# Ranked routing, a written-out first expert iteration, and mixer outputs formed transposed in half lanes

## The reference

```python
e = exp(s - max(s)); o = (e / sum(e)) @ v              # each head, queries in blocks of 128
o_b = g0 * o_cmp + g1 * o_sel + g2 * o_win
merged = g_a*(o_a @ w_br_a) + g_b*(o_b @ w_br_b) + g_c*(o_c @ w_br_c)
```

## Time and profile before

| | us |
|---|---|
| median of 3 runs | 1678.88 |
| the profiled execution | 1675.22 |
| its span | 1673.5 |
| TensorE busy in it | 1590.7 (95%) |
| VectorE busy | 939.6 (56%) |
| ScalarE busy | 654.3 (39%) |
| mean granted TensorE clock | 0.988 |

### The profile page before, as it was taken

How to read it: one execution, slowest core, us unless ns; L and a number is a source line. 1 busy time by engine, 2 the same in 40 slices (tenths; PEclk the granted TensorE clock), 3 DMA queues, 4 the chain that set the end, 5 groups by cost and what they waited for, 6 DMA issues and landing times.

```text
span 1673.5 us, 22371 instructions
## 1 busy us (share of the span) xinstructions
PE 1590.7 (95%) x9359; PEld 1237.3 (74%) x9359; DVE 939.6 (56%) x1374; ACT 654.3 (39%) x960; POOL 27.1 (2%) x89
## 2 busy tenths in 40 slices
PE   5999999989999899999999999999999999999998
PEld 1998655454545377687888899978768878889986
DVE  3876676642222465556675566545466567556653
ACT  2543411111111243556545544335265744543441
POOL 1000010100000000000000000000000000000000
PEclk9999999999999999999999999999999999999999
DMA  9555519979999943333345355545424235435551
GB/s 309 189 186 201 202 52 332 386 289 414 411 423 381 353 142 129 102 137 109 133 152 180 123 192 172 191 154 192 154 76 152 101 130 191 157 130 185 202 181 71
DMA packets 153155, 333.33 MB, mean 199 GB/s; under 512 B 17764, under 2 KB 69222, under 8 KB 140774
## 3 DMA queue, kind: packets, MB, share of 16 engines
q1 hardware_dynamic: 147504, 326.94, 53.9%
q10 hardware_dynamic: 5558, 5.06, 0.9%
HBM read 330.94 MB, written 1.05 MB: 198 GB/s over the span
## 4 chain that ended last, share of the span: by engine, by line
PE 81%; DVE 9%; DMA 4%; ACT 4%; issue 1%; POOL 0%; ACTq 0%; POOLq 0%; DVEq 0%; SPq 0%
PE ps_g L737 19%; PE ps_g L718 15%; PE ps_g L1142 6%; PE ps_g L1282 6%; PE ps_s L1538 4%; PE ps_p L1538 3%; PE ps_o L785 3%; PE ps_g L878 3%; DVE ring_r L2314 2%; PE ps_p L718 2%; PE ps_o L1171 2%; DMA ring<-in_w_mod_dram 1%; PE ps_x L1171 1%; PE ps_p L775 1%; DMA arena<-in_w_up_dram 1%
## 5 line engine op out<-in xcount | busy, mean ns | idle before, releaser
L2314 DVE TENSOR_TENSOR ring_r<-ring,late_w 128x4096 fp32r<-128x4096 f32 (+1 forms) x50 | 216.9, 4339 | 153.3 <-ACT late_w L1876 153.3
L1876 ACT ACTIVATE late_w<-ring 128x4096 fp32r<-128x4096 f32 (+1 forms) x50 | 178.2, 3563 | 126.7 <-PE ps_p L1538 42.8
L737 PE MATMUL ps_g<-hf_high,ring_r 128*128 128x256 f32 x640 | 179.0, 280 | 0.0
L737 PE MATMUL ps_g<-hf_high,late_w 128*128 128x256 f32 x576 | 162.1, 281 | 0.0
L737 PE MATMUL ps_g<-h_t_r,late_w 128*128 128x256 f32 x576 | 161.3, 280 | 0.0
L737 PEld LDWEIGHTS ps_g<-hf_high,ring_r 128*128 128x128 f32 x640 | 122.0, 191 | 0.0
L737 PEld LDWEIGHTS ps_g<-h_t_r,late_w 128*128 128x128 f32 x576 | 108.6, 189 | 0.0
L737 PEld LDWEIGHTS ps_g<-hf_high,late_w 128*128 128x128 f32 x576 | 108.1, 188 | 0.0
L1900 ACT ACTIVATE arena<-arena,neg_max 128x256 f32<-128x256 f32 (+1 forms) x160 | 71.5, 450 | 40.9 <-DVE neg_max L2369 40.9
L1142 PE MATMUL ps_g<-arena 128*64 128x512 f32 x288 | 83.9, 592 | 0.0
L718 PE MATMUL ps_g<-early_w,first_low 128*128 128x512 f32 (+1 forms) x176 | 68.7, 390 | 3.8 <-ACT arena L1862 1.8
(11 more groups left out here) (697 smaller groups left out, 3707.1 us busy)
## 6 DMA issues: line engine op xcount, KB each, us to landing
ring<-in_w_in_dram SPq DMA_DIRECT2D x31, 2048.0 KB, 7.8
ring<-in_w_gate_up_dram SPq DMA_DIRECT2D x44, 1024.0 KB, 7.3
arena<-in_w_down_dram SPq DMA_DIRECT2D x16, 2048.0 KB, 13.1
ring<-in_w_mod_dram SPq DMA_DIRECT2D x10, 2048.0 KB, 11.0
ring<-in_w_down_dram SPq DMA_DIRECT2D x10, 2048.0 KB, 7.9
arena<-in_w_gate_dram SPq DMA_DIRECT2D x16, 1024.0 KB, 13.4
arena<-in_w_up_dram SPq DMA_DIRECT2D x8, 2048.0 KB, 16.1
ring<-in_w_gate_dram SPq DMA_DIRECT2D x8, 2048.0 KB, 14.2
```

Source lines behind the costliest of these rows:

```text
L737: ins = pe.matmul(b.ap[:, (f % 2) * SEQ:(f % 2 + 1) * SEQ], a[:, k, f * P:(f + 1) * P], x[:, k, :], start=k == 0 and i == 0, stop=k == nk ...
L1876: act.activation(high_of(name, rnd)[:, 0:n], ring[:, slot, 0:n], ACT.Copy).then_inc(high_ready.sem, 1)
L2314: dve.tensor_tensor(ring_r[:, slot, 0:n], ring[:, slot, 0:n], high_of(name, rnd)[:, 0:n].bitcast(F32), ALU.subtract).then_inc(low_ready.se ...
```

## The change

It has three parts.

**Routing.** Instead of three searches one after the other, every value is compared with every other of its four ("greater", and "equal" times a fixed mask `before` of earlier indices), and the sums are ranks. A group of rank 0 and experts of rank below 2 give `picked`. Gates are formed from rank 0 and rank 1 later. The slot row is made by a matmul of its own in bank O ahead of the h2 transposes and copied by DVE after `shifted`; loads go to bank G0. Modulation chunk 10 moves ahead of `mod_strips(7)` on PE (bank X) and is copied by ACT, its +1 now added as 1/128 in each partition; chunk 11 moves behind the first gather, and DVE takes it after the gates. ACT's exponential of the logit difference and 11 small DMA issues (`layer_vectors(0)`) move behind `take_tokens`.

**Expert pairs.** Pairs 0 and 1 are written out ahead of PE's loop; the register is loaded behind them. In `expert_pair` the waits for banks O and X stand before the gate products' k = 0 and k = 4, and that for M1 before the up products.

**Mixer outputs.** The output is formed transposed: the values are the stationary operand (64 columns, so half the lanes), the transposed probabilities are moving (128 columns). A second set of four matmuls spreads the reciprocals over the lanes. DVE copies those to SBUF, multiplies, and has the branch output transposed already (`heads_t`), so the 24 transposes go away; ACT and DVE make high and low parts from SBUF. For cmp the probabilities are scaled on DVE before PE transposes them.

```diff
+            claim(O, "slot_row")
+            pe.matmul(O.ap[:, 0:SLOT_TOKENS], ones, tri[:, 0:SLOT_TOKENS], start=True, stop=True).then_inc(O.full, 1)
             for tb in range(TB):
                 turn_block("h2", tb, ...)
...
             residual(1)
-            for i in MOD_LATE:
-                modulation(i)
             pe.wait_ge(picked_ready, 1)
             claim(X, "places")
...
             gather(0, "taken")
-            pe.wait_ge(rounds_ready, 1)
-            n_pairs = pe.value_load(rounds_i[0:1, 1:2], ...)
+            modulation(MOD_LATE[1])
...
-            with pe.Fori(0, last_even, 2) as q:
+            even_and_odd(0)
+            pe.wait_ge(rounds_ready, 1)
+            last_even = pe.value_load(rounds_i[0:1, 3:4], ...)
+            with pe.Fori(2, last_even, 2) as q:
                 even_and_odd(q)
...
                     if step[0] != "cmp":
                         turn_probs("layer", step, l)
                         return
-                    pe.wait_ge(probs.sem, probs.at("layer", step_tag(step), l))
+                    pe.wait_ge(blocks_scaled, len(CMP_STEPS) * l + CMP_STEPS.index(step) + 1)
                     claim(PT, step_tag(step), l)
...
+                def turned_output(step, v):
+                    tag, kbs = step_tag(step), keys_of(step) // P
+                    claim(O, tag, l)
+                    pe.wait_ge(PT.free, PT.nth("layer", tag, l))
+                    for c in range(2):
+                        for b in range(kbs):
+                            for half in range(2):
+                                pe.matmul(O.ap[half * HD:(half + 1) * HD, c * P:(c + 1) * P], v(2 * c + half, b), probs_t[:, 2 * c + half, b, :],
+                                          start=b == 0, stop=b == kbs - 1)
+                    pe.wait_ge(inverse_ready, len(WEIGHED) * l + WEIGHED.index(step) + 1)
+                    inverse = rden[:, MIXER_STEPS.index(step) % 2, 0:4]
+                    for i in range(4):
+                        half, c = i % 2, 2 + i // 2
+                        ins = pe.matmul(O.ap[half * HD:(half + 1) * HD, c * P:(c + 1) * P], inverse[:, i:i + 1].broadcast_to([P, HD]), ident[:, :],
+                                        start=True, stop=True)
+                    ins.then_inc(O.full, 1)
...
-                        pe.matmul(O.ap[:, :], probs_t[:, 0, 0, :], cmp_v[...], start=True, stop=True)
+                        for c in range(KF):
+                            ins = pe.matmul(O.ap[:, c * P:(c + 1) * P], v[:, c * P:(c + 1) * P], probs_t[:, 0, 0, :], start=True, stop=True)
...
             for tb in range(TB):
                 shifted(tb)
+            dve.wait_ge(O.full, O.nth("first", "slot_row"))
+            dve.tensor_copy(slot_row[:, 0, :], O.ap[:, 0:SLOT_TOKENS]).then_inc(O.free, 1)
...
-            first_best(rt[:, :, 0:N_GROUPS], 2, 8)
+            for op, over_groups, over_experts in ((ALU.is_gt, group_beats, beats), (ALU.is_equal, group_ties, ties)):
+                v = rt[:, :, 0:N_GROUPS]
+                st.done(dve.tensor_tensor(square(over_groups), each_row(v), each_column(v), op))
+                for tb in range(TB):
+                    v = of_experts(tb)
+                    st.done(dve.tensor_tensor(over_experts[:, tb]..., each_row(v), each_column(v), op))
+            st.settle()
+            ...                                   # ties times earlier (2), beats plus ties (2), sums (2), settled after each
+            do(dve.tensor_scalar(group_rank[:, :, :], group_rank[:, :, :], 0.5, None, ALU.is_lt))
+            do(dve.scalar_tensor_tensor(grouped(picked[:, :, :]), grouped(rank[:, :, :]), 1.5, chosen, ALU.is_lt, ALU.mult))
+            dve.sem_inc(picked_ready, 1)
...
+                    dve.tensor_tensor(block_scores(n), block_scores(n), over(rden[:, n % 2, :], CMP), ALU.mult).then_inc(blocks_scaled, 1)
...
+                def mixer_inverse(n):
+                    step = MIXER_STEPS[n]
+                    if step[0] == "cmp":
+                        total_blocks(n, step)
+                        return
+                    ...                           # waits for probs; sink added for swa; reciprocal; gate for sel, win
+                    ins.then_inc(inverse_ready, 1)
...
+                    dve.wait_ge(O.full, O.nth("layer", step_tag(step), l))
+                    sums, weight = (O.ap[:, i * SEQ:(i + 1) * SEQ].rearrange(...) for i in range(2))
+                    st.done(dve.tensor_copy(o_tmp[:, :, :], weight))
+                    st.settle()
+                    if step[0] != "win":
+                        dve.tensor_tensor(out_t, sums, o_tmp[:, :, :], ALU.mult).then_inc(O.free, 1)
+                        return
+                    ...                           # win: product to o_tmp, then added
...
                 for n, step in enumerate(MIXER_STEPS):
-                    if step[0] == "cmp":
-                        total_blocks(n, step)
+                    mixer_inverse(n)
                     if n + 2 < len(MIXER_STEPS):
                         mixer_mask(n + 2)
                     mixer_finish(n)
...
                 for name in "abc":
-                    turned_low(f"o{name}", KF, o_low[name], o_high[name], l)
+                    for r in range(2):
+                        dve.wait_ge(x_high.sem, x_high.at("layer", f"o{name}{r}", l))
+                        dve.tensor_tensor(o_low[name][:, 2 * r:2 * r + 2, :], heads_t[name][:, 2 * r:2 * r + 2, :],
+                                          o_high[name][:, 2 * r:2 * r + 2, :].bitcast(F32), ALU.subtract).then_inc(heads_low_ready, 1)
```

More of the change, by code:

```diff
@@ L627, in two_blocks @@
         g_col_ready, last_used = sem("g_col_ready"), sem("last_used")
+        inverse_ready, blocks_scaled, heads_low_ready = sem("inverse_ready"), sem("blocks_scaled"), sem("heads_low_ready")
+        WEIGHED = [step for step in MIXER_STEPS if step[0] != "cmp"]
         bg_tanhed, cmp_tanhed = sem("bg_tanhed"), sem("cmp_tanhed")
@@ L1120, in _ @@
                 b.begin("moe", n)
-            for b in (MO, MX):
-                pe.wait_ge(b.free, b.nth("start", "taken"))
-            last_even = pe.value_load(rounds_i[0:1, 3:4], min_val=PAIRS - 2, max_val=PAIRS * ROUNDS - 2)
             def expert_pair(q, gate_landed, gate_w, up_landed, up_w, last=False):
@@ L1131, in weights_of @@
                     return up_w[e]
-                for b in (MO, MX):
-                    pe.wait_ge(b.free, q * 2 + 1)
+                first = isinstance(q, int) and q == 0
                 claim(M0, "gate", q)
-                claim(M1, "up", q)
                 halves = [slice(e * SLOT_TOKENS, (e + 1) * SLOT_TOKENS) for e in range(2)]
@@ L1140, in expert_pair @@
                     for k in range(KD):
+                        if kind and k == 0:
+                            claim(M1, "up", q)
+                        if kind == 0 and k % 4 == 0:
+                            y = (MO, MX)[k // 4]
+                            pe.wait_ge(y.free, y.nth("start", "taken") if first else q * 2 + 1)
                         for lanes, w in zip(halves, both_w):
@@ L1373, in _ @@
                     mixer_output(n)
-                for name, src in (("a", o_a), ("b", o_b), ("c", o_c)):
-                    if name == "b":
-                        pe.wait_ge(rows.sem, rows.at("layer", "ob", l))
-                    else:
-                        pe.wait_ge(O.free, O.nth("layer", step_tag((SWA_STEPS if name == "a" else MLA_STEPS)[-1]), l))
-                    turn_rows(f"o{name}", [lambda tb, k=k, s=src: s[:, tb, k * P:(k + 1) * P] for k in range(KF)], l)
                 def mem_half(r):
@@ L2021, in _ @@
             copy_block("mg", 1, mg_turned)
-            for i in (6, 7):
-                keep_strips(i)
+            keep_strips(6)
+            b = mod_bank(MOD_LATE[0])
+            act.wait_ge(b.full, b.nth("first", MOD_CHUNKS[MOD_LATE[0]]))
+            act.activation(mod_cols(MOD_LATE[0]), b.ap[:, 0:HALF], ACT.Copy).then_inc(b.free, 1)
+            keep_strips(7)
             for i in (6, 7):
@@ L2211, in _ @@
                 for name in "abc":
-                    turned_high(f"o{name}", KF, o_high[name], l)
+                    if name == "b":
+                        act.wait_ge(rows.sem, rows.at("layer", "ob", l))
+                    else:
+                        act.wait_ge(O.free, O.nth("layer", step_tag((SWA_STEPS if name == "a" else MLA_STEPS)[-1]), l))
+                    for r in range(2):
+                        act.activation(o_high[name][:, 2 * r:2 * r + 2, :], heads_t[name][:, 2 * r:2 * r + 2, :], ACT.Copy).then_inc(x_high.sem, 1)
                 make_high("brb", l)
@@ L2803, in _ @@
                 shifted(tb)
-            dve.sem_inc(alpha_ready, 1)
+            dve.wait_ge(O.full, O.nth("first", "slot_row"))
+            dve.tensor_copy(slot_row[:, 0, :], O.ap[:, 0:SLOT_TOKENS]).then_inc(O.free, 1)
+            st.done(dve.memset(before[:, :, :], 0.0))
+            st.settle()
```

(8 more changed lines are left out.)

187 lines of the change are left out of this document (106 added, 81 removed).

## The result

The changed kernel takes 1707.47 us (median of 5 runs, 1706.38 to 1710.48) against 1678.33 (1677.16 to 1680.25) for the kernel before on the same chip: 1.0174 times the time, 95% interval 1.0159 to 1.0189, so 29.1 us slower (26.7 to 31.7). The direction was forecast; the size was not: 10.5 were summed, and 1707 lies outside the range of 1679 to 1700.

The account below looks back on a forecast made before the run. TensorE (PE), busy 95% of the span, was taken to bound the kernel. Routing −3.4, mixer layers +11.6 and clock +2.3 summed to +10.5: 1685.7 us profiled, 1689 with 3.7 added, range 1679 to 1700.

Parts of the forecast that it names:

- routing: Routing stage: ranks make the pick ready sooner, so the expert gate products start 3.4 us earlier.
- output matmuls: Mixer output steps: half-lane matmuls at 0.12 us each change the steps that PE bounds by −1.3 us a layer.
- cmp waits: Mixer steps 8 and 9: PE's transposition waits 3.4 and 4.3 us for DVE's scaled scores; net +5.9 a layer.
- step 16: Inside output 16 of the mixer, PE waits for DVE's reciprocal: +3.0 us a layer.
- steps 0 and 1: Start of the mixer: DVE work for these steps delays its mask of step 3, for which PE waits: +0.9 a layer.
- behind step 17: From the end of output 17 to the first `w_br_a` product, 2.4 instead of 5.1 us: −2.7 a layer.
- clock: PE's granted clock falls behind the new pauses, counted once a layer: +2.3 us in all, bounds 0 and 10.
- a rival of chance 0.08: Mixer outputs: the array drains at each switch of full and half width, at most some 0.15 us each: 1699; chance 0.08.
- written-out pairs: Expert pairs: iterations otherwise run gapless, so written out or looped is the same: 0, bounds −1.7 and +1.7 us.
- PE does not wait: Mixer steps 8, 9 and 16: DVE would be ahead of PE, leaving −9.6 us, 1669; chance 0.13.

Follow-up runs that it names:

- a_only: The kernel before with the routing by ranks and the written-out pairs alone, mixer steps as before: ratio 0.9986, 2.3 us faster.
- early: The full change with DVE's inverse (for cmp steps sums and scaling) of step n+1 placed ahead of the output of step n: 1671.13 us, 0.9940 of the kernel before.
- filled: The full change with extra identity matmuls on PE in its waits at steps 8, 9, 16 and behind output 17: 1694.57 us, 1.0078 of the kernel before.
- c_only: The kernel before with the mixer outputs formed turned in half lanes alone, routing and expert pairs as before: ratio 1.0167, 28 us slower.
- wide: early with the four half-lane inverse matmuls replaced by two of full width, DVE spreading the inverses first: 0.9977 of the kernel before, 6 us slower than early.
- half_filled: As filled, with half the extra matmuls (6, 9, 5 and 4) in the same waits of the full change: 1.0122 of the kernel before.
- low_a: early with ACT's high and DVE's low half of branch a made ahead of output 17: 1668.23 us, 0.9929 of the kernel before.
- top: low_a with the slot-row copy moved between the two shifted blocks: 0.9936 of the kernel before.
- before_early: The kernel before with only DVE's sums and reciprocals of the cmp steps moved ahead of the output of the step before: ratio 0.9999.
- best: low_a plus wide, the second low half of branch a left behind output 17, slot-row copy between the shifted blocks: 1673.26 us, 0.9961 of the kernel before.
- extra: early with nine extra matmuls between gate and up products of pair 0: first gate product to pair 3's first up product 94.0 us against 91.4.
- full_before: early with one extra full-width matmul ahead of the half-lane matmuls in each of 16 output steps a layer: 0.9988 of the kernel before.
- full_between2: Second run of early with one extra full-width matmul between half-lane value products and half-lane weights in 16 steps a layer: 1.0092 of the kernel before.
- top_filled: top with 20 and 13 identity matmuls where PE waits between the expert pairs and the first layer: 1666.84 us, 0.9925 of the kernel before.

## Why the prediction was wrong

By its terms, for the whole kernel:

| term | predicted | found | from |
|---|---|---|---|
| routing | -3.4 | -2.3 (-4.0 to -0.7) | a_only |
| output matmuls | -2.6 | +3.2 | rows of steps in early |
| cmp waits, step 16, steps 0 and 1 | +19.6 | +19.4 | filled against before |
| behind step 17 | -5.4 | -5.4 | 5.3 before, 2.6 in early |
| clock | +2.3 | +14 to +16 | filled against the full change |
| sum | +10.5 | +29 to +31 | measured +29.1 |

"Waits found": filled's first window is 8.6 above before's (the second 7.5, with a fall of 1.15 in before's); less 1.6 for the outputs, plus 2.7 behind step 17, 9.7. Read singly in the profile after, the new waits are 3.28 + 4.41 + 2.60 + 0.87, less the old ones that they replace (0.56, 0.81 and 0.39 for step 3's mask): 9.4. Early, whose DVE is ahead, also loses the two old pauses of 1.4, but its wait for step 3's mask is 0.78 instead of 0.39; -2.7 + 1.6 - 1.4 + 0.4 is -2.1, its window says -2.5. The terms are good to some 0.4 a layer.

**The clock is the step that failed**, with some 12 to 14 of the 19 us missing. The prediction wrote: "The new pauses are longer (3.4, 4.3, 2.9 a layer), so I count one such fall a layer, +2.3 in all; bounds 0 and six falls of 1.7, 10." The mechanism is the one named, and the row it rested on the earlier trace rows was the right one; the count was not. A row with one fall behind a pause of 1.5, in one layer of two, was taken as the rate for pauses of two and three times that length. In the profile after, no pause of 2.5 or more in the mixer steps passed without a fall, also not the one behind step 17, which the prediction had booked only as a gain. And in layer 2 the two cmp waits cost two falls each. c_only's profile has the same eight pauses of 2.5 and more, a fall behind every one, and there a double one in layer 1 too, behind step 9. Even the upper bound, six, was a count of waits and not of falls. filled shows what stands in the place of that step: with the same waits and PE at work in them, 14.6 us of span are gone from the first mixer window on, and with them ten of the eleven falls.

**The second step that failed is the outputs.** Durations were nearly right: 0.54 for eight half-lane records (0.48 forecast), 1.47 and 1.02 for the two kinds of step (1.44 and 0.96), and -0.6 a layer by them. What was put to a rival of chance 0.08 came true in part (in early against before, the rows under wide): into half width the next record follows at 0.33 instead of 0.23, out of it the transposes start 0.05 late, 0.14 a step and 2.2 a layer. The evidence quoted against it, 64 half-width records with nothing lost ahead of them, is one change among many that nobody timed. The Trainium skill, "TensorEngine Tiling (Array Packing)", section "Tiling Modes", says that a change of tiling mode needs a drain. The rows here show a price, so the rule's direction holds; it is about 0.07 a change in the kernel's own step and 0.16 where a lone matmul stands between two changes.

**Right:** the places, sizes and releasers of the waits at steps 8, 9 and 16 (and 0.87 inside output 1, L3250, for the 0.9 of steps 0 and 1); the routing, step by step, the 0.9 against it among them (0.83), and 3.3 of the 3.4 at the gate products where the clock is alike; the gain behind step 17; that written-out pairs are worth nothing by themselves. The rival "PE does not wait" gave 1669, and removing the waits gave 1671: the price of the waits was right on that side too. That the two totals meet is in part luck: early keeps the 2.2 a layer that leaving and entering half width costs, and is free of the fall that before has in layer 2 and of both old waits.

**Open:** why some falls come in twos; what decides in one kernel that the same pause brings the clock down and in another not; how many falls the routing stage has in an execution, and so whether 2 or 3 us of its gain are left.

## What to carry to other kernels

Price a new wait of a busy engine twice: its length, and what the clock does behind it. Here waits of 19 us cost another 14 to 16, and idle matmuls (of the identity, their result written over) in the very same waits gave those back. Ask of every value that moves to another engine's input when its producer can make it: the change was a loss of 1.7% with the inverse formed one place too late and a gain of 0.6% with one block of DVE's code moved. And count changes of the array's width as work of their own when half-lane matmuls replace full ones in small groups.

## Not expected of the hardware

- A fall of the clock costs up to 1.7 us of PE work. Over the pauses of the mixer steps: none behind 0.2 to 0.4 (8 in filled) and 1.2 to 1.4 (4 in half_filled, 4 in low_a and top); the 1.5 ahead of output 0 has a fall right behind it in 3 of 32 places (before, a_only and before_early, once each); 1.75 and 2.40 in all four of half_filled, but 1.75 after output 17 in neither layer of best; the 2.5 after output 17 in none of four in early and extra, one of two in full_before, both in wide and in full_between2; 2.5 to 4.4 in all sixteen of the full change and c_only. Length alone does not decide: behind 0.8, with thin products following, top and top_filled have two falls in a row. The Trainium skill, "TensorE: Matmul & The Clock Gate", part 1, ties the clock to how busy PE has been recently; filled agrees, with clock 1.00 over both windows.
- A switch between full and half width: 0.14 us for a pair in the output step, 0.32 for a pair around a single matmul.
- Two full-width matmuls behind half-width ones took 0.55, no less than the four half-width ones they replaced (0.54).
